# Recurrent projections reordered, one a level; output gate beside the inversion; first chunk copies W1

## The reference, cut to what matters

```python
prev = jnp.pad(p_rw, ((0, 0), (1, 0), (0, 0)))[:, :T]
p_rw = p_rw + (prev - p_rw) * rwkv_mu
rr, rk, rv, xw, xa, xg = jnp.split(p_rw, ...)
w_log = -jax.nn.softplus(-(rwkv_w0 + jnp.tanh(xw) @ rwkv_w2)) - 0.5
decay = jnp.exp(-jnp.exp(w_log))
a = jax.nn.sigmoid(rwkv_a0 + xa @ rwkv_a2)
g_r = jax.nn.sigmoid(xg) @ rwkv_g2
kk = split_heads(rk * rwkv_k_k)
kk = kk / jnp.maximum(jnp.sqrt(jnp.sum(kk * kk, axis=-1, keepdims=True)), 1e-12)
rk = rk * (1.0 + (a - 1.0) * rwkv_k_a)
...
# S_t = S_{t-1} diag(w_t) - (S_{t-1} kk_t)(kk_t * a_t)^T + v_t k_t^T ;  o_t = S_t r_t
o_r = rwkv7_scan(r_h, split_heads(decay), k_h, v_h, kk, split_heads(a))
...
y_rwkv = (gn + bonus) * g_r
```

## Time and profile before

| what | value |
|---|---|
| three runs | 1794.08, 1797.5, 1800.74 us; median 1797.5 |
| the profiled execution | 1799.55 us, its span 1797.7 us |
| granted clock of TensorE, mean over the span | 0.968 |
| busy | PE 1724.2 us (96%), DVE 879.6, ACT 674.9, POOL 130.2 |

### The profile page before, as it was taken

The page is one execution under the profiler, slowest core; times in us unless marked ns, Lnnn a source line. Parts: engine busy times, 40 slices in busy tenths (PEclk is TensorE's granted clock), DMA queues, the critical chain, the costliest instruction groups (busy, mean ns, idle before and its releaser), DMA issues.

```text
span 1797.7 us, 22270 instructions
## 1 busy us (share of the span) xinstructions
PE 1724.2 (96%) x8756; PEld 1407.5 (78%) x8756; DVE 879.6 (49%) x1169; ACT 674.9 (38%) x1017; POOL 130.2 (7%) x126
## 2 busy tenths in 40 slices
PE   7999999999999899999999999969998899999997
PEld 6777778878778788888888778859986688888886
DVE  5633444633436565444335774665345654444333
ACT  5145664225554333332224543453122433333221
POOL 0001002001001000000004000001330200000000
PEclk9999999999999999999999999965999999999998
DMA  5312213322212132223333211200001222232331
GB/s 195 124 65 71 83 59 96 128 82 71 83 60 83 59 118 94 94 94 97 97 100 129 71 59 48 68 9 1 1 19 47 82 83 94 97 103 92 96 97 56
DMA packets 40744, 143.91 MB, mean 80 GB/s; under 512 B 4816, under 2 KB 4832, under 8 KB 40384
## 3 DMA queue, kind: packets, MB, share of 16 engines
q1 hardware_dynamic: 37008, 130.87, 22.5%
q0 software_dynamic: 2192, 8.73, 1.5%
q10 hardware_dynamic: 1440, 2.88, 0.4%
HBM read 140.37 MB, written 2.10 MB: 79 GB/s over the span
## 4 chain that ended last, share of the span: by engine, by line
PE 79%; DVE 14%; ACT 5%; issue 1%; DMA 0%; ACTq 0%; DVEq 0%
PE bank L449 22%; PE bank L450 21%; PE bank L451 21%; PE bank L431 9%; DVE sb_w_low L1113 3%; DVE sb_E L1113 2%; PE bank L437 2%; DVE sb_near L1500 1%; PE bank L667 1%; PE bank L646 1%; ACT sb_E L1829 1%; PE bank L603 1%; ACT sb_w_high L1829 1%; DVE sb_xg_low L1121 1%; DVE sb_x L1113 1%
## 5 line engine op out<-in xcount | busy, mean ns | idle before, releaser
L1113 DVE TENSOR_TENSOR sb_w_low<-sb_raw,sb_w_high 128x1024 fp32r<-128x1024 f32 (+1 forms) x253 | 311.2, 1230 | 389.7 <-ACT sb_w_high L1829 383.6
L449 PE MATMUL bank<-sb_xg_high,sb_w_high 128*128 128x512 f32 x1176 | 469.5, 399 | 24.7 <-DVE sb_xg_low L1121 15.0
L450 PE MATMUL bank<-sb_xg_low,sb_w_high 128*128 128x512 f32 x1176 | 461.9, 393 | 0.0
L451 PE MATMUL bank<-sb_xg_high,sb_w_low 128*128 128x512 f32 x1176 | 461.8, 393 | 0.0
L1829 ACT ACTIVATE sb_w_high<-sb_raw 128x1024 fp32r<-128x1024 f32 (+1 forms) x253 | 263.2, 1040 | 359.2 <-PE bank L451 328.9
L449 PEld LDWEIGHTS bank<-sb_xg_high,sb_w_high 128*128 128x128 f32 x1176 | 223.1, 190 | 92.2 <-issue 32.3
L451 PEld LDWEIGHTS bank<-sb_xg_high,sb_w_low 128*128 128x128 f32 x1176 | 223.1, 190 | 47.7
L450 PEld LDWEIGHTS bank<-sb_xg_low,sb_w_high 128*128 128x128 f32 x1176 | 223.4, 190 | 44.5
L451 PE MATMUL bank<-sb_h_high,sb_w_low 128*128 128x512 f32 x352 | 136.9, 389 | 0.0
L449 PE MATMUL bank<-sb_h_high,sb_w_high 128*128 128x512 f32 x352 | 136.9, 389 | 0.0
L450 PE MATMUL bank<-sb_h_low,sb_w_high 128*128 128x512 f32 x352 | 136.9, 389 | 0.0
(11 more groups left out here) (333 smaller groups left out, 2131.3 us busy)
## 6 DMA issues: line engine op xcount, KB each, us to landing
sb_raw<-w_ffn_in SPq DMA_DIRECT2D x88, 512.0 KB, 3.3
sb_raw<-w_ffn_out SPq DMA_DIRECT2D x32, 512.0 KB, 3.5
sb_raw<-w_tok SPq DMA_DIRECT2D x24, 512.0 KB, 3.4
sb_raw<-w_mix_f SPq DMA_DIRECT2D x18, 512.0 KB, 3.2
sb_raw<-w_rot SPq DMA_DIRECT2D x16, 512.0 KB, 3.6
sb_raw<-w_qk SPq DMA_DIRECT2D x16, 512.0 KB, 3.3
sb_raw<-w_out SPq DMA_DIRECT2D x16, 512.0 KB, 3.2
sb_raw<-w_ffn_out SPq DMA_DIRECT2D x16, 384.0 KB, 3.1
```

The costliest lines, as they stand in the source:

```text
L449: e.matmul(out, w[0], v[0], start=first, stop=False)
L450: e.matmul(out, w[0], v[1], start=False, stop=False)
L451: return e.matmul(out, w[1], v[0], start=False, stop=last)
L1113: e.tensor_tensor(out, a, b, op).then_inc(*v.up(*signal))
```

## The change

`RWKV_ORDER` = 6, 7, 2, 3, 0, 1, 4, 5 gives the projections' order: decay and gate inputs, output gate, keys, receptance, values. One stands in each of fills 0 to 7. The operand steps are split up and stand in the fills from 1 on instead of the last ones. Key squares go to the still empty values' place in `sb_mixed`, cumulated decays to `sb_square`, and some tiles share other memory. GpSimd's offset and gate operations move from `recurrence` to the end of `inverse`. Chunk 0's "carried" product with a zero state is dropped: U of the first 64 tokens is copied from W1.

```diff
+RWKV_ORDER = (6, 7, 2, 3, 0, 1, 4, 5)
...
-    values, projections = mixer_group(1), mixer_tiles(*range(2, 10))
+    values, projections = mixer_group(1), mixer_tiles(*(2 + f for f in RWKV_ORDER))
...
@@ tensor_engine, mixers @@
         def fill_gla(n):
             if n < 2:
                 next(values_g)
+            if n < 8:
                 next(projections)
...
+            if n == 2:
+                decay_and_gate_in()
+            if n == 4:
+                gate_out()
+                key_norm()
+            if n == 7:
+                p.mark("xg read", MIX_NORM)
+            if n == 8:
+                key_turned()
 
         linear_attention("gla", fill_gla)
-        for _ in operand_prep:
-            pass
+        bonus_sums()
...
@@ tensor_engine, recurrence @@
-            i = take(("carried", c), ("U", c))
             p.wait_ge(*of("S", c))
-            p.wait_ge(*of("W2T", 3))
...
+            if c:
+                i = take(("carried", c), ("U", c))
+                p.wait_ge(*of("W2T", 3))
...
@@ vector_engine, mixers @@
-            tt(m.tmp, m.cum, m.sigma, ALU.subtract, "sigma before")
+            tt(before, m.cum, m.sigma, ALU.subtract, "sigma before")
...
+        def keys():
+            v.wait_ge(*of("xg read", MIX_NORM))
             for f in range(2):
                 v.wait_ge(*of("key turned", f))
                 stt(kk[:, f, :], rk[:, f, :], mem.col("rwkv_k_k", f), bank("key turned", f)[:, :], ALU.mult, ALU.mult,
                     "key scaled", f)
...
         def fill_gla(n):
             if n < 2:
                 next(values_g)
...
+            if n == 0:
+                finish_hgrn()
+            if n == 4:
+                decay_sums()
+            if n == 5:
+                key_floor()
+            if n < 8:
                 next(projections)
...
+            if n == 8:
+                keys()
+            if n == 9:
+                receptance()
...
@@ vector_engine, recurrence @@
         small, out_r = mem.small, m.y_tok["rwkv"]
+        v.wait_ge(*of("W1", 3))
+        ts(m.U[0:64, 0, :], m.W1[0:64, 0, :], 1.0, None, ALU.mult, ALU.bypass, "U", 0)
         memset(m.S, 0.0, "S", 0)
...
@@ scalar_engine, mixers @@
         def fill_gla(n):
             if n < 2:
                 next(values_g)
...
+            if n == 0:
+                finish_hgrn()
+            if n == 1:
+                decay_in()
+            if n == 2:
+                bend_gate("gla")
+            if n == 3:
+                gates()
+            if n == 4:
+                key_squares()
+            if n == 5:
+                decay_exps()
+                gate_out()
+            if n < 8:
                 next(projections)
...
+            if n == 7:
+                key_spread()
...
@@ gpsimd_engine, inverse @@
-    def recurrence(m):
-        fence("recurrence")
         bonus = mem.small[:, 112:128]
+        g.wait_ge(*of("y made", "gla"))
+        g.wait_ge(*of("tokB", TT - 1))
...
         tt(m.g_tok, m.g_tok, over_tiles(m.rows[:, 0, :]), ALU.mult, "gate ready")
+
+    def recurrence(m):
+        fence("recurrence")
         pool_squares(NEXT_NORM[MIX_NORM])
```

More of the change, by code:

```diff
@@ L865, in operand_steps, with gate_out @@
                     group(banks[i][:, :], [(m.lora[r, 0, blk(f)], m.mixed[r, 6, :])], what + " in", f)
[L866 to L872, removed]
+        def gate_out():
             for half in range(2):
@@ L878, in operand_steps, with key_norm, key_turned @@
                           "gate out", half)
+        def key_norm():
+            i = take(("key norm",), ("key floored",))
+            p.wait_ge(*of("key squares"))
+            for t in range(TT):
+                for f in range(2):
+                    at = 4 * t + 2 * f
+                    group(banks[i][:, at:at + 2], [(m.mixed[:, 4 + f, blk(t)], mem.table("same_head")[:, 0:P:64])],
+                          "key norm")
+        def key_turned():
             for f in range(2):
@@ L1766, in recurrence @@
             t, r = c // 2, slice(64 * (c % 2), 64 * (c % 2) + 64)
[L1767 to L1769 removed]
+            if c:
+                v.wait_ge(*of("carried", c))
+                tt(m.U[r, t, :], bank("carried", c)[r, 0:G], m.W1[r, t, :], ALU.add, "U", c)
             next(filler, None)
@@ L2201, in rwkv_steps @@
         def rwkv_steps():
-            for f in range(8):
+            for k, f in enumerate(RWKV_ORDER):
                 use()
@@ L2228, in operand_steps, with key_squares, decay_exps, key_spread @@
                     "g tok", half)
-            yield
+        def key_squares():
+            a.wait_ge(*of("rwkv mixed", 3))
+            for f in range(2):
+                act(m.mixed[:, 4 + f, :], m.mixed[:, 2 + f, :], "key squares", func=ACT.Square,
+                    scale=mem.col("rwkv_k_k", f))
+        def decay_exps():
             a.wait_ge(*of("sigma before"))
             act(m.eB, m.cum, *STEP, func=ACT.Exp, scale=-HALF_E)
-            act(m.rE, m.cum, *STEP, func=ACT.Exp, scale=HALF_E)
-            act(m.tmp, m.tmp, "rwkv exps", func=ACT.Exp, scale=-HALF_E)
-            yield
-            yield
-            a.wait_ge(*of("bonus in"))
-            act(small[:, 112:128], bank("bonus")[:, 0:16], "bonus")
-            yield
-        projections, operand_prep = rwkv_steps(), operand_steps()
+            act(m.cum, m.cum, *STEP, func=ACT.Exp, scale=HALF_E)
+            act(m.sigma, m.sigma, "rwkv exps", func=ACT.Exp, scale=-HALF_E)
+        def key_spread():
+            a.wait_ge(*of("xg read", MIX_NORM))
+            a.wait_ge(*of("key inverse"))
+            act(heads(flat(m.kI)), small[:, 176:192].unsqueeze(2).to_broadcast([P, 16, 64]), "key spread")
+        projections = rwkv_steps()
         def fill_gla(n):
@@ L2263, in mixers @@
         finish_gla = linear_attention("gla", fill_gla)
-        for _ in operand_prep:
-            pass
+        a.wait_ge(*of("bonus in"))
+        act(small[:, 112:128], bank("bonus")[:, 0:16], "bonus")
         preset("X", m.X, "factors read")
```

115 lines of the change are left out of this document (39 added, 76 removed).

## The result

| | before | change |
|---|---|---|
| median of the runs | 1797.5 us | 1806.6 us (1804.89 to 1807.38) |
| profiled execution, its span | 1799.55, 1797.7 us | 1806.31, 1804.5 us |
| mean granted clock | 0.968 | 0.968 |

A forecast was written before the change was run, and what follows sets the result against it. One-projection levels were taken as paced by VectorE and ScalarE: +9.5 us to the mixed products, -3.0 in the recurrence, +6.5 in sum, so 1804.0 us on the median of 1797.5; range 1787 to 1812.

The forecast's parts named there:

- The levels: Passes of the linear_attention loop, one projection each, paced by VectorE and ScalarE at 9.1 us, lengthened by added operand work.
- Rival 2: Levels 1, 2 and 4: ScalarE is early enough to hide its operand work; 11.6 us less, 1792.4 us; chance 0.05.
- The step of 5.4 us for the keys: VectorE's five key products stand ahead of the mark the mixed products wait for, moving it from 1210.2 to 1215.6 us.
- The clock: Granted clock stays 0.50 through mixed products, bonus sums and inversion's first products, times unchanged; 0.18 for it being up earlier.
- The recurrence: First chunk, after the inversion: copying W1 and moving GpSimd's offset chain together save 3.0 us.
- GpSimd's contention: First chunk: VectorE's weight subtraction and fade run slowly beside GpSimd; moving its chain saves 1.85 and 1.4 us.
- the W1 copy: First chunk: VectorE copies W1, costing 0.4 us, and drops an add with its gap, saving 0.5 us.
- bound of -4.5: Recurrence's best case, in us, if the output products also lose their low-clock stretch after the 2 us wait.
- The fence: Recurrence's start waits for GpSimd's chain until 1329.1 us instead of VectorE's last W2T copy at 1328.7; +0.4 us.
- rival 3: At the recurrence's fence GpSimd's chain, stretched beside other engines, becomes the bound; +3.1 us, 1807.1 us; chance 0.10.
- rival 4: Two ScalarE table switches on the path, to silu and sigmoid, cost 2.6 us more through draining; 1806.6 us; chance 0.03.
- Rival 1: Clock is up before the mixed products, speeding them, bonus sums and inversion's first products; 16.8 us less, 1787.2; chance 0.18.

The follow-up runs named there:

- late: The change with ScalarE's operand work in fills 1 to 5 moved behind each level's weight conversion and token-shift copy; 1807.56 us, ratio 1.0055.
- mix: The change with ScalarE's operand work dealt out over three places of each level, some before and some behind the token-shift copy; 1792.65 us, ratio 0.9966.
- best: mix_warm with VectorE's key products moved behind the mark the mixed products wait for, and 5, 1 and 1 fillers; 1786.38 us, ratio 0.9928.
- mix_warm: mix with 6 unread TensorE products added ahead of the turned keys, last pair products and mixed products; 1786.4 us, ratio 0.9925.
- b_pool: The kernel before with only GpSimd's offset chain moved to the end of the inversion; ratio 0.9996.
- b_w1: The kernel before with only the first chunk's W1 copy in place of the carried product; ratio 1.0003.
- b_warm: The kernel before with 15 unread TensorE products added in its own holes ahead of the mixed products; 1799.19 us, ratio 0.9999.
- gram_warm: mix_warm with 2 more unread products ahead of each head's products at the inversion's start, 8 in all; 1796.38 us, ratio 0.9988.
- a_warm: The change with 12 unread TensorE products added ahead of the turned keys, last pair products and mixed products; 1792.03 us, ratio 0.9963.

## Why the prediction was right

**The levels.** By its steps: level 1 starts at 1134.89 (forecast 1134.5), the levels take 11.28, 14.00, 12.87, 14.77, 9.51 and 9.10 us (11.3, 14.0, 12.9, 14.7, 9.5, 9.1), the last factors are ready at 1210.43 (1210.2). Mixed products start at 1216.01 (1215.8), +9.3 us against the near products' start (+9.5). late and mix show that this was the right cause, and that the forecast's account of it was too short: it let `w_low` pay for levels 1, 2 and 4 and named TensorE's bank in passing. Taking the work out of `w_low`'s way alone put the mixed products 4.8 us further off. Rival 2 is excluded by `w_low`'s waits of 2.32, 5.00 and 4.01 us. The step of 5.4 us for the keys was the last wait, as forecast (1.96 us in TensorE's timeline), but ScalarE's last copy stood close behind it, and best shows that at most 1.6 us hung on it in mix_warm.

**The clock.** 0.50 over mixed, bonus and first products, as forecast (0.18 had gone to the other case). The first mixed products still ran at 1.00, since the clock had come up once more at some 1213 us, and this gave 0.85 us.

**The recurrence** was forecast at -3.0 and gave -3.5. The size was nearly right, its making was not. The sum subtracted 1.85 and 1.4 for GpSimd's contention and set the W1 copy at -0.5 and +0.4; b_pool and b_w1 show 0.85 and -0.13 us at chunk 1 for the one and the other alone, 3.5 together. What holds the rest is TensorE's 2.02 us wait and the low clock behind it, which the forecast named only in its bound of -4.5. The fence cost nothing instead of 0.4: beside nothing but VectorE's copies from banks GpSimd's chain takes 9.97 us (1326.86 to 1336.83), not 11.3, and ends before VectorE's last W2T copy (1337.31). So rival 3 was excluded. No step had the 1.65 us of the last column either, output products that met a low clock.

**The table switch.** ScalarE's timeline of the change in level 1:

```profile
1136.35 1.06 ACT L1844 ACTIVATE sb_E<-sb_E 128x1024 f32<-128x1024 f32 x1 [3.95 <-DVE sb_E L1123]
1137.42 1.28 ACT L1844 ACT_TABLE_LOAD   x1
1138.71 1.06 ACT L1844 ACTIVATE sb_v_gla<-sb_v_gla 128x1024 f32<-128x1024 f32 x1
```

The load starts as the exp ends and silu starts 1.29 us after it. That agrees with the earlier trace rows and not with the 2.66 us with drain of the Trainium skill ("ScalarE: Activation LUTs", What ACT_TABLE_LOAD costs); rival 4 was excluded.

**The number.** On the profiled execution the forecast was 1806.05, measured 1806.31 us. On the medians it was 1804.0 and 1806.6: the profiled run of before lay 2.05 us above its median, that of the change within 0.3 us of its own. That the total came within 0.3 us is luck: the steps were off by -0.2 (levels and keys), -0.85 (mixed products), +0.1 (rest of the inversion), -0.5 (recurrence) and +1.65 (last column), and these cancel. The forecast held 9 us for the least that can be told from no change; the measured interval, 5.0 to 9.3 us, is narrower and clear of zero. Rival 1's price of 16.8 us would have been too high by most of its 7 us for the first products.

## What to carry to other kernels

Where two engines pass a loop's work between them, list for each step that is put ahead of a shared one who waits behind it, through operands and through the banks it holds; moving it behind the first waiter can hand the wait to the next. Price edits at a join of two chains together, never one by one. A clock gained by filling a hole is worth only what the next waits leave of it: read the granted clock behind the gain too.

## What the runs showed of the hardware that was not expected

- The granted clock fell to 0.50 with TensorE busy 8.96 of 9 us (b_warm, 1208 to 1217 us). It was 0.50 over most of the inversion's first 22 us, products without a gap, in all kernels but gram_warm, where it was 1.00 with two idle products of 512 columns ahead of each head's. What decides the moment stays open: it fell at some 1228 us in a_warm, as the inversion's first products began, and at some 1210 us in b_warm, 2.5 us into the mixed products.
- GpSimd's chain and VectorE slow each other (before and b_w1 against b_pool and the change): VectorE's weight subtraction of 0.96 became 2.8 to 3.2 us and its fade of 0.43 became 1.8, GpSimd's first four operations 2.69 became 3.35. But VectorE's operations that read a bank took the same beside it (the state's subtraction 0.42, the four `sb_y_low` of 3.31).
